# The low part of a quarter of the gate weights: a plain load and a GpSimd subtraction in place of an adding load

## What is computed

```python
h = rms_norm(hs, norm_mix[l])
z = h @ w_in[l]
u_ssm, q, k, v, gates = jnp.split(z, splits, axis=-1)
y_a = s5_mixer(u_ssm, ...)
y_b = windowed_gqa(q, k, v, attn_sink[l])
g = jax.nn.sigmoid(gates + b_gate[l]).reshape(bsz, L, N_BRANCH, D_MODEL)
merged = g[:, :, 0] * (y_a @ w_proj_ssm[l]) + g[:, :, 1] * (y_b @ w_proj_attn[l])
hs = hs + merged @ w_out[l]
hs = hs + peer_ffn(rms_norm(hs, norm_ffn[l]), ...)
```

## Time and profile before

| | us |
|---|---|
| runs | 2123.21, 2126.53, 2128.21 (median 2126.53) |
| the profiled execution, its own time | 2124.16 |
| its span, first to last instruction | 2122.3 |
| first and last gate matmul | 219.5 and 541.7 |
| PE busy in the span | 1772.6 (84%) |
| DVE busy | 1292.7 (61%) |
| ACT busy | 485.2 (23%) |
| POOL busy | 811.4 (38%) |
| mean granted TensorE clock | 0.976 |

### The profile page before, as it was taken

How to read it: one execution, slowest core, us unless ns; L and a number is a source line. 1 busy time by engine, 2 the same in 40 slices (tenths; PEclk the granted TensorE clock), 3 DMA queues, 4 the chain that set the end, 5 groups by cost and what they waited for, 6 DMA issues and landing times.

```text
span 2122.3 us, 25130 instructions
## 1 busy us (share of the span) xinstructions
PE 1772.6 (84%) x8384; PEld 1117.3 (53%) x8384; DVE 1292.7 (61%) x2427; ACT 485.2 (23%) x991; POOL 811.4 (38%) x686
## 2 busy tenths in 40 slices
PE   7987889999899999978978987777777776777776
PEld 5976788888799885524534542223322222322222
DVE  4545767867445446566566676676675665665654
ACT  5332556555434321010110110001000000000001
POOL 1041222222054015455455454433643643643431
PEclk9998899999999999999999999999999999999999
DMA  4430899999645569999999999999999999999997
GB/s 190 162 120 20 206 204 219 221 226 215 219 172 184 178 222 422 422 421 422 422 422 422 422 420 421 422 421 409 415 421 416 418 417 410 401 413 423 422 421 296
DMA packets 106678, 695.00 MB, mean 327 GB/s; under 512 B 11856, under 2 KB 11856, under 8 KB 30928
## 3 DMA queue, kind: packets, MB, share of 16 engines
q0 software_dynamic: 92160, 604.02, 74.9%
q1 hardware_dynamic: 14432, 89.90, 11.5%
HBM read 691.78 MB, written 2.10 MB: 327 GB/s over the span
## 4 chain that ended last, share of the span: by engine, by line
DMA 39%; PE 38%; issue 8%; DVE 7%; POOL 3%; ACT 3%; DVEq 0%; POOLq 0%; ACTq 0%; SPq 0%
DMA uv<-u_tab,eid 30%; PE ps L1639 14%; DMA halves<-W 8%; PE ps L1283 3%; PE ps L1282 3%; PE ps L1284 3%; PE ps L1589 2%; POOL uv L438 2%; DVE uv L1220 2%; PE ps L1573 1%; PE ps L1572 1%; PE ps L1275 1%; PE ps L1571 1%; PE ps L1379 1%; POOL uv L435 1%
## 5 line engine op out<-in xcount | busy, mean ns | idle before, releaser
L1639 PE MATMUL ps<-uv,dg 128*128 128x512 f32 x2048 | 957.6, 614 | 267.3 <-DVE dg L1226 257.7
L1220 DVE CUSTOM_DVE_ANT_0 uv<-uv,xn 128x2048 f32<-128x2048 f32 x256 | 587.1, 2293 | 378.2 <-DMA uv<-u_tab,eid 359.8
L1639 PEld LDWEIGHTS ps<-uv,dg 128*128 128x128 f32 x2048 | 379.9, 193 | 822.7 <-issue 466.5
L438 POOL DMA_INDIRECT uv<-v_tab,eid x256 | 276.3, 1079 | 593.7 <-PE ps L1639 328.7
L435 POOL DMA_INDIRECT uv<-u_tab,eid x256 | 348.5, 1361 | 198.8 <-issue 184.0
L714 ACT ACTIVATE ga<-av 128x1 f32<-128x1 f32 x256 | 51.9, 203 | 1184.7 <-DVE av L1220 1184.7
L1379 PE MATMUL ps<-hH,halves 128*128 128x256 f32 x512 | 152.4, 298 | 28.3 <-DMA halves<-W 28.0
L768 DVE TENSOR_TENSOR low_ring<-ring,wh 128x2048 fp32r<-128x2048 f32 x43 | 101.1, 2356 | 77.0 <-ACT wh L458 76.9
L1380 PE MATMUL ps<-hLx,halves 128*128 128x256 f32 x512 | 147.0, 287 | 0.0
L1381 PE MATMUL ps<-hH,halves 128*128 128x256 f32 x512 | 146.9, 287 | 0.0
L407 POOL DMA_DIRECT2D halves<-W x64 | 55.6, 868 | 224.4 <-ACT halves L541 224.4
(11 more groups left out here) (279 smaller groups left out, 2307.7 us busy)
## 6 DMA issues: line engine op xcount, KB each, us to landing
ring<-W SPq DMA_DIRECT2D x72, 1024.0 KB, 4.9
halves<-W POOLq DMA_DIRECT2D x128, 512.0 KB, 7.0
xn<-x SPq DMA_DIRECT2D x4, 1024.0 KB, 10.6
uv<-u_tab,eid POOLq DMA_INDIRECT x256, 15.4
uv<-v_tab,eid POOLq DMA_INDIRECT x256, 14.2
bwt<-bw SPq DMA_DIRECT2D x8, 256.0 KB, 7.0
cwt<-cw SPq DMA_DIRECT2D x8, 256.0 KB, 8.2
out<-xn SPq DMA_DIRECT2D x4, 512.0 KB, 5.3
```

The source lines that it names most:

```text
L438: pool.indirect_dma_start(uv[:, s, 1, :], None, v_tab, at).then_inc(s_vv[s], 16)
L1220: nc.vector.tensor_tensor_reduce(uv[:, j % UV, 0, :], uv[:, j % UV, 0, :], xn[:, T, :], 1.0, 0.0, ALU.mult, ALU.add, av[:, hh, j:j + 1]).t ...
L1639: ins = nc.tensor.matmul(ps[:, 4 * T + n, :], dg[:, j % 2, :], uv[:, j % UV, 1, n * 512:(n + 1) * 512], start=False, stop=last and i == 2 ...
```

## The change

For the odd half of each gate tile, the adding load and the minus-high copy shrink from 8 blocks to the first 4. The last 4 blocks, [128, 512], are loaded plainly by SP (`quarter`), with its order of loads written out instead of the loop, into one of two slots in the first half of ring slot 0. GpSimd subtracts the high part from them in place (`rest_quarter`; `quart_low` lies over the same bytes), right after it has issued the adding load of the odd half and ahead of the next casting load. TensorE waits for that subtraction four blocks into the odd half and takes the low part of those blocks from `quart_low`. The slots are laid out anew: two quarters, four high halves, two low first halves, two low third quarters. The even halves are as before.

```diff
+QUART = KT // 4
...
-        halves, = over(("halves", [P, 2 * RING, D // 2]))
+        quart_low, high_halves, low_first, low_third = over(("quart_low", [P, 2, QUART * P]), ("high_halves", [P, RING, D // 2]),
+                                                            ("low_first", [P, 2, KT // 2 * P]), ("low_third", [P, 2, QUART * P]))
...
+        quart = ring[:, :, :].rearrange("p r d -> p (r d)")[:, 0:2 * QUART * P].rearrange("p (s n) -> p s n", s=2)
+
         def gate_hi(q):
-            return halves[:, q, :]
+            return high_halves[:, q, :]
 
         def gate_lo(q):
-            return halves[:, 4 + q, :]
+            return low_third[:, q // 2, :] if q % 2 else low_first[:, q // 2, :]
...
-            with sp.Fori(0, CT // 2) as b:
-                for cc in range(2):
-                    sp.wait_ge(s_bu, PPC * (2 * b + cc) + PPC)
-                    sp.dma_start(bwt[:, cc, :, :, :].rearrange("p d r s -> p (d r s)"),
-                                 bw[bass.ds(2 * b + cc, 1), :, :].rearrange("a p n -> (a p) n")).then_inc(s_bw[cc], 16)
-                    sp.wait_ge(s_cpl, 8 * (2 * b + cc) + 8)
-                    sp.dma_start(cwt[:, cc, :, :, :].rearrange("p i r c -> p (i r c)"),
-                                 cw[bass.ds(2 * b + cc, 1), :, :].rearrange("a p n -> (a p) n")).then_inc(s_cw[cc], 16)
+            def quarter(g):
+                sp.wait_ge(s_wdone, RING + (W_Q + RING + 1 if g < 2 else W_GATE + g - 2 + 1))
+                sp.dma_start(quart[:, g % 2, :], W[W_GATE + g, :, (KT - QUART) * P:]).then_inc(s_gp[g % 2], 16)
+
+            for ct in range(CT):
+                cc = ct % 2
+                sp.wait_ge(s_bu, PPC * ct + PPC)
+                sp.dma_start(bwt[:, cc, :, :, :].rearrange("p d r s -> p (d r s)"), bw[ct, :, :]).then_inc(s_bw[cc], 16)
+                sp.wait_ge(s_cpl, 8 * ct + 8)
+                sp.dma_start(cwt[:, cc, :, :, :].rearrange("p i r c -> p (i r c)"), cw[ct, :, :]).then_inc(s_cw[cc], 16)
+                for g in range(max(0, PPC * ct - 4), PPC * ct):
+                    quarter(g)
+            for g in range(GATES - 4, GATES):
+                quarter(g)
...
             def rest_half(h):
+                n = (QUART if h % 2 else KT // 2) * P
                 pool.wait_ge(s_gn, h + 1)
-                pool.dma_start(gate_lo(h % 4), half_weights(h), accum_op=ALU.add).then_inc(s_ga[h % 4], 16)
+                pool.dma_start(gate_lo(h % 4), half_weights(h)[:, 0:n], accum_op=ALU.add).then_inc(s_ga[h % 4], 16)
+
+            def rest_quarter(g):
+                pool.wait_ge(s_gp[g % 2], 16 * (g // 2) + 16)
+                pool.wait_ge(s_gc[(2 * g + 1) % 4], 16 * ((2 * g + 1) // 4) + 16)
+                pool.tensor_tensor(quart_low[:, g % 2, :], quart[:, g % 2, :], gate_hi((2 * g + 1) % 4)[:, (KT // 2 - QUART) * P:], ALU.subtract
+                                   ).then_inc(s_gq, 1)
...
                 rest_half(h)
+                if h % 2:
+                    rest_quarter(h // 2)
...
-                nc.scalar.activation(gate_lo(q), gate_hi(q), ACT.Copy, scale=-1.0).then_inc(s_gn, 1)
+                n = (QUART if half else KT // 2) * P
+                nc.scalar.activation(gate_lo(q), gate_hi(q)[:, 0:n], ACT.Copy, scale=-1.0).then_inc(s_gn, 1)
...
+                wq = quart_low[:, t % 2, :].rearrange("p (m c) -> p m c", c=P)
                 for m in range(8):
                     k = 8 * half + m
+                    if half and m == 8 - QUART:
+                        pe.wait_ge(s_gq, SPC * b + t + 1)
+                    low_part = wq[:, m - 8 + QUART, :] if half and m >= 8 - QUART else wl[:, m, :]
...
-                    ins = nc.tensor.matmul(ps[:, t % 2, 0:SEQ], wl[:, m, :], hH[:, k, META:L], start=False, stop=(k == KT - 1))
+                    ins = nc.tensor.matmul(ps[:, t % 2, 0:SEQ], low_part, hH[:, k, META:L], start=False, stop=(k == KT - 1))
```

More of the change, by code:

```diff
@@ L60 @@
 KEPT = SEQ // 2 + 1
+QUART = KT // 4
+LOWS = 2 * KT - 2 * QUART
 def build(nc, W, keys, par, bw, cw, meta, x, gffn, gfin, u_tab, v_tab, out):
@@ L267, in build @@
         s_gh = sem("s_gh")
+        s_gp = [sem(f"s_gp{q}") for q in range(2)]
+        s_gq = sem("s_gq")
         s_gel, s_sgg, s_glu, s_sig, s_ya = sem("s_gel"), sem("s_sgg"), sem("s_glu"), sem("s_sig"), sem("s_ya")
```

## The result

The changed kernel took 2109.05 us (median of 7 runs, 2101.66 to 2112.14), the kernel before 2124.33 (7 runs beside them, 2118.53 to 2128.21). The ratio is 0.9925, 95% interval 0.9908 to 0.9942: 16 us faster, 12 to 20 by the interval. The forecast was 11 faster, 2115, with its own range from 2109 to 2121: the result lies at the lower end of it. The profiled execution has a span of 2110.0 us.

What follows compares the result with a forecast made beforehand. The gate stage was taken as bound by DMA work: 0.44 us less per gate, 0.47 at a share of 0.93, is 15.1 us over 32 gates, less a quarter 11. Forecast 2115 us, range 2101 to 2131, the forecast's own 2109 to 2121.

Steps and rivals of the forecast that it cites:

- The price of the short adding load: Odd half's 512-column adding load: 1.47 us of DMA work instead of 2.72, saving 1.25 us per gate.
- Net work per gate: Gate stage DMA work: 9.65 - 1.25 + 0.81 = 9.21 us per gate, 0.44 less.
- The rival that it costs by rows: Short adding load stays at up to 2.72 us, making the kernel 28 us slower, 2154; chance 0.04.
- the one that all kinds cost alike by bytes: Transfers cost by bytes whatever their kind, so time would be 2126; chance 0.20 together with gaps eating the gain.
- The quarter off for missed leads: Gate stage: some leads missed, engines stand briefly, so 15.1 us of gain becomes 11, 0.34 us per gate.
- GpSimd's hold of the odd cast: Subtraction delays the next odd cast to 2.16 us after the adding load; 1.3 us of lead remains, costing nothing.
- the shrinking lead of the even adding load: Even adding load arrives 3.2 us after its cast's end, with 3.4 us of work before it instead of 4.6.
- buys lead, no time: ScalarE's odd-half copy falls from 1.07 to some 0.55 us, saving no time while DMA work binds.
- Nothing waits long for TensorE: Gate stage: nothing waits long for TensorE or VectorE, and everything waits for DMA.
- The subtraction: GpSimd's 128x512 subtraction takes 1.29 us and can hold VectorE 41 us over 32 gates, hidden in idle time.
- the slower rival: Quarter load reaches GpSimd late, holding the next odd cast: 12 us slower, 2138; chance 0.11.
- TensorE as the bound: Plain loads run in gaps, 1.25 us per gate returns, TensorE gives up 25.3 us of waits: about 2100; chance 0.12.

Runs made afterwards that it cites:

- the DMA part alone: Changed kernel with ScalarE's time on an odd half put back to about 1.05 us by an extra 192-column copy and a semaphore; ratio 0.9949 against the kernel before.
- three kernels without it: Changed kernel with the subtraction put after the next cast, left out, or given to VectorE; ratios 0.9916, 0.9927 and 0.9932 against the kernel before.
- the doubled load: Changed kernel with every quarter tile loaded twice, one load after the other, GpSimd waiting for the second; ratio 1.0130 against the kernel before.
- at twice the count: Changed kernel with every half's last 512 columns loaded plainly and GpSimd subtracting after the next cast, 64 subtractions; ratio 0.9963 against the kernel before.

## Why the prediction was nearly right

- **The bound.** DMA work is the main bound of the gate stage of the kernel before: the DMA part alone gave 11 of the 16 us, and one more load, on the changed kernel, took all 16 back for 0.78 us per gate. It is not the only one: those 16 us are two thirds of what that load would cost if DMA work alone set the time.
- **The price of the short adding load.** Taken as 1.47 us, it is 1.36, in proportion to its bytes. Net work per gate fell by 0.57 us and not 0.44. The rival that it costs by rows is out, and so is the one that all kinds cost alike by bytes: 256 KB took 1.36 us added and 0.80 plain.
- **The quarter off for missed leads.** The full worth of the heavier saving is 0.57 / 0.93 x 32 = 20 us, and the DMA part alone gave 11: nearly half was missed, not a quarter. The prediction's own 11 came from a saving that was too small and a loss that was too small; that they met at 11 is luck. The loss was not in GpSimd's hold of the odd cast (three kernels without it are no faster, and in 21 of 30 places the cast waited for TensorE anyway). The prediction had also named the shrinking lead of the even adding load and a ScalarE queue that is not always free; TensorE's waits for `low_first`, 14.3 us, fit that.
- **ScalarE's shorter copy "buys lead, no time".** This is the step that failed. With the copy doubled the changed kernel is 11 us slower, clear of noise, so ScalarE's time on the odd half does count there. The copy's share in the change itself is the gap between the DMA part alone and the whole, some 5 us, likely but not sure, and as said above a lower granted clock stands beside it as a rival. The chain that the prediction read the earlier trace rows ran through ScalarE at every turn.
- **The clock.** The prediction has no term for it. 6.7 of the 16 us of the stage are TensorE's busy time, at a clock of 0.99 where it was 0.97. Whether that is a result of the shorter waits or a cause of its own stays open.
- **"Nothing waits long for TensorE."** Its own rows say otherwise: GpSimd's casts waited 34.1 us for it. A cast needs a slot that TensorE is done with, so TensorE is part of the round.
- **The subtraction.** 1.29 us was a good price; the record of 1.61 us is longer than the time until GpSimd's next issue. On VectorE it cost 1.2 us per gate, 38 us, where 41 was named; its worth in time nothing, as forecast, and not covered for long: at twice the count it cost time.
- **The quarter load** landed in 5.1 us, sooner than bwt and cwt, and GpSimd never waited for it; the slower rival fell on that, and the doubled load shows that its mechanism was sound.
- **TensorE as the bound** was given an eighth of the chance. It is not yet the bound here. With every half's last quarter loaded plainly and VectorE subtracting it was nearly reached (2.7 us idle of 289.9). With the expert loop moved that kernel took 2097 us, below the 2100 that the prediction gave for this bound: the prediction had TensorE's waits to give, and its busy time fell too.
- **Still open.** From the last gate matmul to the end the profiled executions need 1580.6 us before and 1584.6 after, and most kernels with a shorter stage some 1584. 2.7 us of it pass ahead of the product with `w_out`, which starts 132.0 us after the last gate matmul before and 134.7 after. No run was made on that.

## What to carry to other kernels

Price each kind of DMA from its own queue's busy share before moving bytes: here an adding load cost 1.7 times a plain one of the same bytes, and the work saved, not the bytes, gave the time. When a bound is lightened, what was "only lead" on the other engines of the same round can start to count, so leave room for it in the range. After any edit compare the untouched stages too: here a shift of the code took back 13 of some 30 us.

## What the hardware showed

- Beside GpSimd's subtraction of 128x512 VectorE's operations took longer: L977 1977 ns where it was 679, and L959, a copy of 16 columns, 808 where it was 164; 1.2 us for each subtraction in all. The subtraction took 1582 to 1646 ns in the changed kernel; where it followed a cast, 1312 ns at the median and up to 2059.
- Worked out from the queues' busy shares: an adding load of 512 KB took 2.72 us of all 16 engines, one of 256 KB 1.36, a casting load of 512 KB 1.90 (two of them alone), a plain one of 256 KB 0.80.
- Ahead of VectorE's expert loop the program has 1095 VectorE instructions in the kernel before and in the changed one (counted in the built programs). With 101 more VectorE stood 34.4 us in 8 places ahead of one operation of the loop, up to 5.6 us each, for nothing that the profile shows, beside 31 instruction loads. With none more, with 53 more (the kernel with VectorE's one subtraction) and with 256 more it stood 11 to 12 us in 2 to 4 places, beside 21 or 22 loads.
